# Where a decoder trunk sums the squares of x, where the root of their mean lies, and when x is stored

## The reference

```
x = x + 0.5 * rmsnorm(swiglu(rmsnorm(x, g[0]), ffn1...), g[1])
x = x + rmsnorm(mix(rmsnorm(x, g[2])), g[3])
x = x + 0.5 * rmsnorm(swiglu(rmsnorm(x, g[4]), ffn2...), g[5])

rmsnorm(x, g) = x * rsqrt(mean(x*x over the features) + EPS) * g
swiglu(x)     = (silu(x @ w_gate) * (x @ w_up)) @ w_down      # 1024 -> 2688 -> 1024
```

## Time and profile before

| what | value |
|---|---|
| median of 3 runs | 2165.89 us |
| the profiled execution's own time | 2166.59 us |
| its span, first to last instruction | 2164.9 us |
| TensorE busy | 2106.8 us, 97% |
| VectorE busy | 1362.9 us, 63% |
| ScalarE busy | 1000.1 us, 46% |
| GpSimd busy | 800.8 us, 37% |
| mean granted clock of TensorE | 0.992 |

### The profile page before, as it was taken

How to read it: one execution, slowest core, us unless ns; L and a number is a source line. 1 busy time by engine, 2 the same in 40 slices (tenths; PEclk the granted TensorE clock), 3 DMA queues, 4 the chain that set the end, 5 groups by cost and what they waited for, 6 DMA issues and landing times.

```text
span 2164.9 us, 45498 instructions
## 1 busy us (share of the span) xinstructions
PE 2106.8 (97%) x18864; PEld 2051.7 (95%) x18864; DVE 1362.9 (63%) x2147; ACT 1000.1 (46%) x2027; POOL 800.8 (37%) x645
## 2 busy tenths in 40 slices
PE   8899999999999999999998999999999999899999
PEld 8899999999899989999988999999998899899998
DVE  5999701666457899951289994026654678999313
ACT  5466522534344546652254664235243545566422
POOL 3421274534324431135433113444332354311442
PEclk9999999999999999999999999999999999999999
DMA  6233443322233423343232334333223233233432
GB/s 186 59 99 98 125 114 92 86 71 66 64 90 102 130 76 101 98 127 97 82 125 77 103 103 129 104 90 81 70 60 98 57 116 116 84 98 101 130 92 78
DMA packets 395245, 209.79 MB, mean 97 GB/s; under 512 B 31920, under 2 KB 385472, under 8 KB 395040
## 3 DMA queue, kind: packets, MB, share of 16 engines
q1 hardware_dynamic: 394896, 206.84, 33.8%
q10 hardware_dynamic: 144, 0.06, 0.0%
HBM read 189.18 MB, written 17.67 MB: 96 GB/s over the span
## 4 chain that ended last, share of the span: by engine, by line
PE 80%; DVE 12%; ACT 2%; DMA 2%; issue 2%; POOL 1%; SPq 0%; DVEq 0%; ACTq 0%
PE ps L1026 45%; PE ps L1038 28%; PE ps L1307 1%; DMA w_raw<-in_ffn_w_gate 1%; DVE xn_lo L2241 1%; POOL w_lo L893 1%; DVE stage L2415 1%; DVE x_ops L2436 1%; DMA w_raw<-in_ffn_w_up 1%; DVE x_ops L2433 1%; DVE x_r L2438 1%; DVE spare L2482 1%; DVE numer L2864 1%; DVE x_ops_f L2418 1%; ACT w_hi L1649 1%
## 5 line engine op out<-in xcount | busy, mean ns | idle before, releaser
L893 POOL TENSOR_TENSOR w_lo<-w_raw,w_hi 128x512 fp32r<-128x512 f32 (+1 forms) x440 | 585.1, 1339 | 775.1 <-ACT w_hi L1649 773.3
L1026 PE MATMUL ps<-xn_hi,w_hi 128*128 128x272 f32 x2496 | 575.2, 297 | 34.6 <-POOL w_lo L893 15.3
L1026 PE MATMUL ps<-xn_hi,w_lo 128*128 128x272 f32 x2496 | 557.7, 290 | 0.0
L1026 PE MATMUL ps<-xn_lo,w_hi 128*128 128x272 f32 x2496 | 557.2, 290 | 0.0
L1649 ACT ACTIVATE w_hi<-w_raw 128x512 fp32r<-128x512 f32 (+1 forms) x440 | 264.4, 605 | 617.9 <-PE ps L1026 462.6
L1026 PEld LDWEIGHTS ps<-xn_hi,w_hi 128*128 128x128 f32 x2496 | 410.3, 191 | 58.9 <-issue 32.5
L1026 PEld LDWEIGHTS ps<-xn_lo,w_hi 128*128 128x128 f32 x2496 | 411.7, 191 | 0.3
L1026 PEld LDWEIGHTS ps<-xn_hi,w_lo 128*128 128x128 f32 x2496 | 410.2, 191 | 0.0
L1038 PE MATMUL ps<-x_ops,w_hi 128*128 128x272 f32 x1920 | 368.9, 288 | 0.3
L1038 PEld LDWEIGHTS ps<-x_ops,w_hi 128*128 128x128 f32 x1920 | 302.0, 189 | 1.7 <-ACT rstd L1882 1.2
L2223 DVE TENSOR_TENSOR acc<-acc,gs 128x544 f32<-128x544 f32 (+1 forms) x45 | 35.2, 782 | 319.6 <-ACT gs L1717 319.0
(11 more groups left out here) (399 smaller groups left out, 3529.4 us busy)
## 6 DMA issues: line engine op xcount, KB each, us to landing
w_raw<-in_ffn_w_down SPq DMA_DIRECT2D x160, 256.0 KB, 2.9
w_raw<-in_w_in SPq DMA_DIRECT2D x120, 256.0 KB, 2.9
w_raw<-in_ffn_w_gate SPq DMA_DIRECT2D x76, 256.0 KB, 2.9
spare_f<-in_ffn_w_gate SPq DMA_DIRECT2D x64, 256.0 KB, 2.9
spare_f<-in_ffn_w_up SPq DMA_DIRECT2D x64, 256.0 KB, 2.9
w_lo_f<-in_ffn_w_up SPq DMA_DIRECT2D x56, 256.0 KB, 2.8
w_raw<-in_ffn_w_up SPq DMA_DIRECT2D x48, 256.0 KB, 2.9
x_aside<-x SPq DMA_DIRECT2D x16, 544.0 KB, 4.8
```

The costliest lines, as they stand in the source:

```text
L893: pool.tensor_tensor(w_lo[:, q % RING, 0:m], w_raw[:, q % RAW, 0:m], w_hi[:, n % RING, 0:m].bitcast(F32), ALU.subtract).then_inc(w_split, 1)
L1026: mm = pe.matmul(pair(p)[:, a, :], w, z[:, half(a)], start=(k == 0 and j == 0), stop=(k == chunks - 1 and j == 2))
```

## The change

It does five things.

- The sum of squares is kept in `pair(3)`; only the last of the seven additions writes to `acc` in SBUF, from where TensorE reads it.
- The matmul by ones is issued at the end of unit 3, not in the middle of unit 4, which is 24 matmuls earlier. This holds for the mixers too.
- ScalarE makes the root after the high parts of blocks 9 to 11; those of 12 and 13 come after it. In an FFN it writes the root twice: first over `pair(3)` (`rstd_lent`), then into `rstd` (`rstd_ready`).
- VectorE reads the root from `pair(3)` in `gate(0)`, `gate(1)`, all of `x_mix` and in `up(0)` to `up(3)`, and starts on `rstd_lent`. From `gate(2)` on the gates read `rstd`. The first product A11, which overwrites bank 6, waits also until these have read it.
- SyncE stores x between the loads of blocks 9 to 16, a store after every second load, and issues the first pair loads after that.

The rest of the diff takes out code for an option that was off (`BY_POOL` was empty).

```diff
-            put(0)
-            sync_load(sp, n_up + 9)
-            put(1)
-            sync_load(sp, n_up + 10)
-            put(2)
-            sync_load(sp, n_up + 11)
-            put(3)
-            sync_load(sp, n_up + 12)
+            for c in range(4):
+                sync_load(sp, n_up + 9 + 2 * c)
+                put(c)
+                sync_load(sp, n_up + 10 + 2 * c)
             for j in (0, 2, 3):
                 sync_load_pair(sp, l, which, 0, j)
-            for i in range(13, 16):
-                sync_load(sp, n_up + i)
+                sync_load(sp, n_up + 17 + j // 2 + j % 2)
             sp.wait_ge(rstd_ready, v + 1)
             sync_load_pair(sp, l, which, 0, 1)
-            for i in range(16, UP_PLAIN):
+            for i in range(20, UP_PLAIN):
...
-                pe_unit(pe, i % 3, n_up + 2 * i, (lambda c: c == 3 and pe_pre_sum(pe, v)) if i == OPEN + 1 else None)
+                pe_unit(pe, i % 3, n_up + 2 * i, (lambda c: c == 7 and pe_pre_sum(pe, v)) if i == OPEN else None)
...
                 if w == 0:
                     pe.wait_ge(rstd_ready, v + 1)
+                    pe.wait_ge(x_normed, 8 * (2 * l + which + 1))
+                    pe.wait_ge(h_scaled, f0 + LENT_TILES)
                     pe.wait_ge(up_read, g0 + PLAIN_TILES - 1)
...
-                if t == OPEN + 1 and c == 3:
+                if t == OPEN and c == 7:
                     pe_pre_sum(pe, v)
...
             act.activation(halves(std[:]), pair(3), ACT.Ln, bias=eps_t[:, 0:1], scale=1.0 / D).then_inc(ln_done, 1)
             act.wait_ge(ln_done, 3 * v + 1)
+            if v % 3 != 1:
+                act.activation(pair(3), halves(std[:]), ACT.Exp, scale=-0.5).then_inc(rstd_lent, 1)
             act.activation(rstd[:], std[:], ACT.Exp, scale=-0.5).then_inc(rstd_ready, 1)
...
-            for b in range(9, 14):
+            for b in range(9, 12):
                 act_high(act, n + b)
             act_pre(act, v)
+            for b in range(12, 14):
+                act_high(act, n + b)
...
-                dve.tensor_tensor(acc[:], x_sq[:, 0, :] if c == 1 else acc[:], x_sq[:, c, :], ALU.add).then_inc(x_summed, 1)
+                dve.tensor_tensor(halves(acc[:]) if c == DC - 1 else pair(3), halves(x_sq[:, 0, :]) if c == 1 else pair(3),
+                                  halves(x_sq[:, c, :]), ALU.add).then_inc(x_summed, 1)
...
-                    dve.tensor_tensor(g, g, rstd[:], ALU.mult).then_inc(gate_scaled, 1)
+                    dve.tensor_tensor(halves(g), halves(g), pair(3), ALU.mult).then_inc(gate_scaled, 1)
                     return
+                if t == 2:
+                    dve.wait_ge(rstd_ready, v + 1)
...
-                dve.tensor_tensor(g, g, rstd[:], ALU.mult).then_inc(h_scaled, 1)
+                dve.tensor_tensor(halves(g), halves(g), pair(3) if t < LENT_TILES else halves(rstd[:]), ALU.mult).then_inc(h_scaled, 1)
...
-                                             halves(rstd[:]), ALU.mult, ALU.mult).then_inc(x_normed, 1)
+                                             pair(3), ALU.mult, ALU.mult).then_inc(x_normed, 1)
...
-            dve.wait_ge(rstd_ready, v + 1)
+            dve.wait_ge(rstd_lent, done0 + 1)
```

More of the change, by code:

```diff
@@ L49, in program @@
     PLAIN_TILES = 6
+    LENT_TILES = 4
     PAIRS = FC - PLAIN_TILES
@@ L321, in h_tile @@
             return xn_hi[:, t - EARLY_H, :], xn_lo[:, t - EARLY_H, :]
[L323 to L328, removed]
         def x_operand(k, c):
@@ L409, in program @@
         w_low = sem("w_low")
-        w_low_pool = sem("w_low_pool")
+        rstd_lent = sem("rstd_lent")
         z_kept = sem("z_kept")
@@ L919, in up @@
                 low(4)
[L921 to L930, removed]
                 for t in range(PLAIN_TILES - 1, FC - 1):
                     low(t)
-                    if t < FC - 2:
-                        for k in BY_POOL:
-                            w_lower(t - PLAIN_TILES + 2, k)
                 splits(n_up + UP_ITEMS, n_up + UP_ITEMS + RING)
@@ L1159, in product @@
                 def product(k, bank, before_chunk=None):
-                    pe.wait_ge(w_low_pool if k in BY_POOL else w_low, lows_to(done, k))
+                    pe.wait_ge(w_low, PRODUCTS * done + k + 1)
                     pe_product(pe, n + k, w_slot(w, k, after), k, bank, k in (A11, A22MINUS21, A12), before_chunk)
@@ L2478, in w_lower @@
                 slot = w_slot(w, k, after)
-                if k in BY_POOL:
-                    return
                 dve.wait_ge(w_hi_ready, n + 1)
```

## The result

The changed kernel took 2136.09 us in the median of 4 runs (2134.72 to 2137.53), against 2165.03 us in 4 runs of the kernel before. The ratio is 0.9865, with a 95% interval of 0.9848 to 0.9882. That is 28.9 us faster. The forecast was 2143, with a range of 2133 to 2155.

A forecast was written before the change was run, and what follows sets the result against it. VectorE was taken to bound the four FFN openings. 4 x 5.6 us there plus 0.4 for the mixers, 22.8 us off 2166.6, gave 2143.8, less 0.7 for the median: forecast 2143, range 2133 to 2155 for 8 in 10.

The forecast's parts named there:

- The bound: In FFN openings VectorE sets A11's time, `gate(0)` plus 51 us; it can move 11.5 us before TensorE binds.
- The sum in PSUM: Additions of squares at 0.72 us, 0.82 with the wait, ending 2.2 us ahead of the matmul by ones.
- The root: In the fourth FFN opening, high 11 sets Ln and the lent root comes 6.5 us earlier.
- Silu: Before `up(0)`: silu(0) ends at 1813.15, VectorE is ready at 1813.1; `up(0)` moves 6.4 us earlier.
- The collision with split 13: Beside the last steps of `x_mix(0)`, GpSimd's split slows VectorE: 1.0 us off each opening, bounds 0 and 2.2.
- Reading the root from PSUM: In VectorE's readers it costs the same as from SBUF, 0.71 against 0.72 us: nothing.
- The stores: In SyncE's queue: store 1 is down by 1809.2, before `x_mix(0)` writes x at 1812.2; costs nothing.
- Rival B: FFN openings: loads ahead of their store land in 2.9 us, matmul by ones sets Ln, no split interferes; 2136 us, 16%.
- C: Openings: loads stay late (5.8 and 5.2 us), silu 2.5 us later, A11 falls to half-clock TensorE; 2150 to 2155, 20%.
- D: Additions into PSUM take 1.86 us, so TensorE waits 4.6 us in each of six openings; slower, 2173 us, 6%.
- TensorE's clock: Half clock behind unit 9 might lose 2.8 us, making TensorE later than VectorE by 1.1 us at worst.
- The mixers: Both mixers lose their waits for the root: 0.4 us gained in all, bounds 0 and 1.

The follow-up runs named there:

- e3: The changed kernel with the high parts of blocks 12 and 13 ahead of the root again in ScalarE's queue; 2150.51 us.
- e4: The changed kernel with the matmul by ones back in the middle of unit 4, in FFNs and mixers; 2145.59 us.
- e6: The kernel before with only the new order of stores and loads in SyncE's queue; 2153.27 us.
- e8: The kernel before with only the high parts of blocks 12 and 13 moved behind the root; 2158.48 us.
- e5: The changed kernel without the lent root: one Exp into `rstd` in SBUF, which all readers use; 2145.73 us.
- after_again: The changed kernel run once more, unaltered, in a later set; 2137.73 us.
- e11: The kernel before with the high parts of blocks 12 and 13 behind the root, and the root lent in PSUM; 2148.90 us.
- e2: The changed kernel with the stores of x and the pair loads back in the old order of SyncE's queue; 2145.15 us.
- e9: The changed kernel with the matmul by ones 12 matmuls earlier, and the root ahead of the high part of block 11 too; 2137.28 us.

## Why the prediction was right, and where it was off

- **The bound.** Right in the main. `w_lower(0, 0)` ended 7.2, 5.4, 7.2 and 7.0 us earlier, and the edits that moved `gate(0)` by over 2 us in every opening moved the time (e3, e4, e6, e8). So did e5, which only made VectorE's own work longer. But a sign of being wrong that I had named did come: in three of four openings it isn't VectorE that releases A11. TensorE gets there 0.7, 0.6 and 1.6 us after `w_lower(0, 0)` has ended, where 0.25 is the usual. I had kept up to 1.1 us an opening for this in the range and nothing in the sum. A11 came 7.2, 5.0, 6.8 and 5.7 us earlier, 24.7 in all. Another 3.3 us of the FFN stages came behind A11, for which the sum had no term. TensorE idles 4.1 us there over the four stages, and 6.8 before. So what TensorE's lateness took at A11 came back behind it.
- **The sum in PSUM.** 0.73 us an addition, 0.72 forecast, and 2.2 us ahead of unit 3's end, as forecast. What I missed is that the sum also stops slowing GpSimd. Splits 6 to 8 take 4.24 us in place of 5.20, and load 11 goes out 1.0 us sooner, counted from unit 3. With the sum back in SBUF (e1) it goes out 0.8 us later again. GpSimd's timeline after (before, the same three start at 1796.97 and take 5.20):

```profile
1772.11 4.24 POOL L882 TENSOR_TENSOR w_lo<-w_raw,w_hi 128x512 fp32r<-128x512 f32 x3 [13.03 <-ACT w_hi L1626]
```

- **The root.** Set by high 11 in three openings, as forecast; in the first it was the matmul by ones, and in the profile of after_again in the first three. `gate(0)` came 6.1, 6.0, 7.2 and 7.0 us earlier (mean 6.6; the forecast was 6.5 in the fourth). The landing of load 11 was 5.0, not 4.35, but it had been issued sooner. Two errors met, and that the root was hit to 0.5 us is partly luck.
- **Silu.** I expected 0.1 us of wait. There was none, since load 13 took 2.9 us and not 4.05.
- **The collision with split 13.** This is the term of the sum that was mis-sized. I took 1.0 us off each opening. It did occur, and at the size I gave it: up to `up(0)` VectorE took 0.3, 1.8, 0.9 and 0.9 us longer (1.34 in place of 0.44 us on one instruction in `x_mix(0)`, in the fourth). But from `up(0)` to `w_lower(0, 0)` it took 1.3, 1.2, 0.9 and 0.9 us less, 43.1 to 43.5 in place of 44.4: in the fourth opening two instructions went from 1.77 to 1.28 and from 1.07 to 0.72. With the root back in SBUF (e5) this stretch takes 44.4 us again and both instructions are long again. So it is the root's place, the next point, that cancelled the collision. The net is 0, and the stretch from `gate(0)` to `w_lower(0, 0)` came out at 47.8, 49.5, 48.9 and 48.9 us against 48.9. With a net of 0 in place of 1.0 the sum is 26.8 us, and `w_lower(0, 0)` ended 26.8 us earlier over the four openings. The median's 28.9 and the stages' 27.9 are near it.
- **Reading the root from PSUM.** I called it nothing, on equal durations of 0.71 and 0.72, and in another paragraph I assumed that such readers aren't hit. The durations are equal only without GpSimd beside them. e5 and e11 put some 9 to 10 us on it. More than half of that the sum had taken for granted, since the readers up to `up(0)` weren't to be hit. The rest, 4.2 us behind `up(0)`, stood nowhere in it and made up for the collision. So that the sum came out near is in part luck.
- **The stores.** I costed the edit at nothing as a cover question and put its worth into the landing times. It is 9 to 12 us by itself (e2, e6). The cover held: the second store landed 0.9 to 2.9 us after unit 3, in each opening before `gate(0)` began.
- **Rival B** had the number, 2136, and part of the mechanism. Its bare 2.9 us for a load directly ahead of a store came for load 13 in all four openings (2.9, 3.2, 2.9 and 2.9) and for load 9 in three (2.9, 3.0, 3.0, and 4.5 in the fourth). It didn't come for load 11, which has the first store ahead of it, still under way: 4.4, 5.4, 4.9 and 5.0. Load 11 is the one that sets high 11. So in three openings the matmul by ones didn't set Ln, and `gate(0)` came 6.6 us earlier and not 7.3. Nor was its "no split in the way" so. The root's place and what came behind A11 made up for both, and that the rival has the number is luck. The Trainium skill (DMA: Bandwidth & Descriptors, Queues, rings and completion order) has a semaphore wait for earlier writes of its engine, not for later ones. The trace agrees for loads 11 and 13 and for load 9 in three openings. Load 9 in the fourth, 4.5 us with no store ahead of it, differs; it took 3.9 to 4.9 in the other profiles with this order of stores too. What delays it was not found.
- **Rivals C and D.** Of C only A11's fall to TensorE came: load 11 landed after 4.4 to 5.4 us and not 5.8, and silu wasn't late. D is refuted by 0.73 us an addition.
- **TensorE's clock.** The half clock behind unit 9 came in three openings, for 3.4, 3.4 and 6.8 us (the window of 0.61 above holds the last). Over the four openings TensorE runs 13.7 us at half clock, where it ran 23.9 before. It cost little, since what comes late at A11 is made up behind it.
- **The mixers.** I took 0.4 us for both. The first took 321.2 us before and after, and the second differs by 1.8, which is within what mixers vary by. No run shows the 0.4.

The parts don't add up. Undone one at a time they cost 6.6, 9.0, 14.4, 9.5 and 9.6 us, 49 in all, for a gain of 29. Three of the five (the matmul by ones, the highs and the stores) feed one wait, the root's, where the latest input counts, and each uncovers the next.

What stays open: the 4 us outside the FFN stages in the two profiles. Up to the first unit 3 the changed kernel itself took 39.8 and 41.3 us, and mixers come out at 321.2 or near 322.8 without order. After_again makes chance likely for the first of these. For the share of it in the medians there is no run.

## What to carry to other kernels

When a wait is moved, look at what the work it let pass will now run beside. The move of two high parts gave 6.5 us and, with one operand put out of the second engine's way, 15.4. An operand's place has a price that its own duration doesn't show. It is seen in the spread of a line's durations (725/1628/1858), not in its least value. In e9 new collisions took back most of what an earlier root gave. And a chain with three inputs needs all three moved: read from the profile which is latest, move it, and read again.

## What the runs showed of the hardware that I had not expected

- A VectorE instruction of 128x544 with both tensor inputs in SBUF takes up to 1.8 us beside GpSimd and not 0.72. With one input in PSUM it took 0.73 in all 36 additions, beside the same splits, in the 30 that write to PSUM and the 6 that write to SBUF.
- It goes both ways: three GpSimd splits took 5.20 us beside additions in SBUF and 4.24 beside those in PSUM.
- A 256 KB load issued directly ahead of a 544 KB store on the same queue landed after 2.9 to 3.2 us in seven of eight cases (loads 9 and 13; no store ahead, or one that landed within 0.3 us of the load's issue), and after 4.5 in the eighth. With a store issued 2.1 to 2.8 us ahead of it and another load between (load 11), it landed after 4.4 to 5.4. Which of these two delays it wasn't taken apart, and why the eighth took 4.5 is open.
